# Attention start-up and the unit of the roots: one copy and the weight splits change places, and the odd query projection, sums and key spread of the first pair come later

## What is computed

```
q = (rms_norm(q_a, q_a_norm_g) @ w_uq).reshape(b, l, 16, 96)
kv = (rms_norm(kv_a, kv_a_norm_g) @ w_ukv).reshape(b, l, 16, 64 + 64)
k_nope, v = split(kv); k = concat([k_nope, broadcast(k_rope_raw)])
q = rms_norm(q, q_norm_g); k = rms_norm(k, k_norm_g)        # per head and token
q, k = rope on the last 32 features of each
s = q @ k.T * 96 ** -0.5, causal; p = softmax(s); out = p @ v
g_ssd, g_mla = split(sigmoid(gates + gate_b))               # gates = h @ w_in
x = x + (g_ssd * (y_ssd @ w_ssd_proj) + g_mla * (out @ w_mla_proj)) @ w_o
```

## Time and profile before

| | us |
|---|---|
| median of 3 runs | 1775.56 |
| the profiled execution's own time | 1777.97 |
| its span, first to last instruction | 1776.2 |
| PE busy | 1687.0 (95%) |
| DVE busy | 1069.2 (60%) |
| ACT busy | 814.2 (46%) |
| POOL busy | 628.5 (35%) |

### The profile page before, as it was taken

One profiled execution on the slowest core, in us unless ns is written; L12 is line 12 of the kernel. 1 busy time (PEld: TensorE's weight loads), 2 busy tenths in 40 slices (PEclk: granted clock), 3 DMA queues, 4 the chain that ended last, 5 costly groups with the idle time before them and its releaser, 6 DMA issues.

```text
span 1776.2 us, 22696 instructions
## 1 busy us (share of the span) xinstructions
PE 1687.0 (95%) x7979; PEld 1321.7 (74%) x7979; DVE 1069.2 (60%) x1659; ACT 814.2 (46%) x1344; POOL 628.5 (35%) x275
## 2 busy tenths in 40 slices
PE   7999899999999799999997999999999999999999
PEld 5688677767787688776675876677678788888887
DVE  6599377676526677777778026676656656666300
ACT  5432366656334355566564225554643344444310
POOL 4244211232444144344353332221224344444442
PEclk9999899999998899999999999999999899999999
DMA  6233221221432233211112221111123223233331
GB/s 203 62 95 95 77 66 48 60 72 49 153 103 87 90 96 107 66 53 36 48 46 85 76 79 48 47 52 45 60 85 108 82 93 96 94 94 96 105 95 59
DMA packets 40119, 142.72 MB, mean 80 GB/s; under 512 B 4696, under 2 KB 5176, under 8 KB 39648
## 3 DMA queue, kind: packets, MB, share of 16 engines
q1 hardware_dynamic: 37600, 131.96, 24.3%
q10 hardware_dynamic: 2432, 9.59, 1.5%
HBM read 137.31 MB, written 4.21 MB: 80 GB/s over the span
## 4 chain that ended last, share of the span: by engine, by line
PE 77%; DVE 13%; ACT 5%; issue 4%; POOL 0%; ACTq 0%; DVEq 0%; POOLq 0%
PE bank L700 16%; PE bank L702 15%; PE bank L701 15%; PE bank L1290 4%; PE bank L1289 4%; PE bank L1288 4%; PE bank L1184 1%; PE bank L751 1%; PE bank L753 1%; PE bank L752 1%; PE bank L1096 1%; PE bank L841 1%; PE bank L1205 1%; PE bank L859 1%; PE bank L1193 1%
## 5 line engine op out<-in xcount | busy, mean ns | idle before, releaser
L591 POOL TENSOR_TENSOR w_lo<-w_raw,w_hi 128x1024 fp32r<-128x1024 f32 x243 | 590.9, 2435 | 1108.8 <-ACT w_hi L1310 963.3
L700 PE MATMUL bank<-u_hi,w_hi 128*128 128x512 f32 x776 | 328.9, 424 | 14.0 <-DVE taps L2285 9.0
L1310 ACT ACTIVATE w_hi<-w_raw 128x1024 fp32r<-128x1024 f32 x199 | 208.3, 1055 | 226.9 <-PE bank L702 184.6
L702 PE MATMUL bank<-u_hi,w_lo 128*128 128x512 f32 x776 | 307.5, 396 | 0.0
L701 PE MATMUL bank<-u_lo,w_hi 128*128 128x512 f32 x776 | 307.2, 396 | 0.0
L700 PEld LDWEIGHTS bank<-u_hi,w_hi 128*128 128x128 f32 x776 | 148.4, 191 | 77.4 <-issue 30.5
L702 PEld LDWEIGHTS bank<-u_hi,w_lo 128*128 128x128 f32 x776 | 148.1, 191 | 32.7
L701 PEld LDWEIGHTS bank<-u_lo,w_hi 128*128 128x128 f32 x776 | 148.7, 192 | 29.9 <-issue 3.4
L1288 PE MATMUL bank<-u_hi,w_hi 128*128 128x512 f32 x320 | 124.5, 389 | 0.0
L1289 PE MATMUL bank<-u_lo,w_hi 128*128 128x512 f32 x320 | 124.5, 389 | 0.0
L1290 PE MATMUL bank<-u_hi,w_lo 128*128 128x512 f32 x320 | 124.5, 389 | 0.0
(11 more groups left out here) (463 smaller groups left out, 3548.6 us busy)
## 6 DMA issues: line engine op xcount, KB each, us to landing
w_raw<-weights SPq DMA_DIRECT2D x243, 512.0 KB, 3.6
xt<-x_t SPq DMA_DIRECT2D x8, 256.0 KB, 6.2
hank<-bias_dram ACTq DMA_DIRECT2D x8, 256.0 KB, 3.1
xt<-x_t ACTq DMA_DIRECT2D x1, 2048.0 KB, 9.3
h_dram<-h_res ACTq DMA_DIRECT2D x1, 2048.0 KB, 7.0
h_res<-h_dram ACTq DMA_DIRECT2D x1, 2048.0 KB, 7.7
out<-h_res SPq DMA_DIRECT2D x8, 256.0 KB
p_val<-p_t ACTq DMA_DIRECT2D x1, 512.0 KB, 11.4
```

Source lines behind the costliest of these rows:

```text
L591: pool.tensor_tensor(w_lo[:, j, :], w_raw[:, j, :], w_hi[:, j, :].bitcast(F32), ALU.subtract).then_inc(w_lo_ready, 1)
L700: pe.matmul(o, hi, xh, start=(i == 0), stop=False)
L702: mm = pe.matmul(o, lo, xh, start=False, stop=(i == n - 1))
L1310: act.activation(w_hi[:, c % RING, :], w_raw[:, c % RING, :], ACT.Copy).then_inc(w_hi_ready, 1)
```

## The change

PE's program for pair 0: the odd query projection stands behind 7 instead of 4 steps of the last output tile; its sums, the key sums and the odd sums follow after 9 and 12 steps instead of 4 and 10; the first value tile now stands ahead of the key spread, and the first gate tile has two steps instead of one before the second value tile. ACT computes one exponential of a constant behind the roots of pair 0, which brings the table in there. In the loop ACT leaves out the copy of unit i = 3 wherever a further pair follows, and DVE makes that copy ahead of the reciprocal of the roots. The split of unit i = 2 moves to unit i = 4, in every pair.

```diff
@@ PE, pair 0 @@
-            column_tile(last_out, of_y, part=(0, 4))
+            column_tile(last_out, of_y, part=(0, 7))
             project_query(1)
+            column_tile(last_out, of_y, part=(7, 9))
             query_sums(0)
-            column_tile(last_out, of_y, part=(4, 10))
+            column_tile(last_out, of_y, part=(9, 12))
             key_sums(0)
             query_sums(1)
-            column_tile(last_out, of_y, part=(10, 16))
+            column_tile(last_out, of_y, part=(12, 16))
+            row_tiles(st["v"][0:4], of_kn)
             key_spread(0)
-            row_tiles(st["v"][0:4], of_kn)
-            column_tile(gate0, of_u2, part=(0, 1))
+            column_tile(gate0, of_u2, part=(0, 2))
             row_tiles(st["v"][4:8], of_kn)
-            column_tile(gate0, of_u2, part=(1, 3))
+            column_tile(gate0, of_u2, part=(2, 3))
@@ ACT @@
             head_norms(0)
+            act.activation(norm_col[:, 2, 1:2], vec("eps"), ACT.Exp)
             scan_out(7)
...
-                head_turned(n)
-                if i == 2:
+                if i != 3 or not more:
+                    head_turned(n)
+                if i == 4:
                     after(st["head_q"][2 * p + 3] if more else st["mix_gate"][2 * p])
@@ DVE @@
                     if i == 3:
+                        dve.wait_ge(x_turn, n + 1)
+                        if n >= 4:
+                            dve.wait_ge(x_sum, n // 2 - 1)
+                        dve.tensor_copy(turned_x[:, n % 4, 0:(ti + 1) * P],
+                                        bank[6][:, 0:(ti + 1) * P]).then_inc(x_turned_out, 1)
                         head_scales(p + 1)
```

## The result

The changed kernel takes 1782.48 us (median of 20 runs, 1775.85 to 1787.6), the kernel before 1775.16 us (20 runs, 1772.8 to 1777.74): a ratio of 1.0038, 95% interval 1.003 to 1.0046. It is slower by 7.3 us where 1.4 us faster was forecast, and lies outside the range. The profiled execution took 1784.96 us, its span is 1782.8 us (before 1776.2), its mean granted clock 0.976.

What follows compares the result with a forecast made beforehand. PE, with 77% of the chain of waits, was taken as the bound. Start-up -3.6, clock +1.4, loop 0, last pair +0.85 sum to -1.35 us: 1774.2 from 1775.56, range 1770.5 to 1779.0.

Steps and rivals of the forecast that it cites:

- Odd query projection: Start-up, PE: three more output steps cover the 1.88 us q_s wait; start at 1039.8, 3.4 us of clock loss spared.
- Key spread and v_tok: Start-up: spread at 1053.0, second value tile at 1058.6, 2.5 us earlier, PE waiting about 3.1 us for v_tok.
- Fall of the clock behind that wait: Second value tile: clock down for 3.4 us after the v_tok wait, costing 1.4 us.
- clock stays up: Rival, start-up: no fall of the clock behind the 3.1 us v_tok wait; 1772.8 us, chance 0.15.
- Exponential ahead: Start-up, ACT: early table load removes PE's 0.92 us probs_x wait and more; gain 1.1 us, between 0.9 and 1.6.
- Loop, k_s for turned_x: Attention loop, PE: the 3.0 us of turned_x waits turn into k_s waits, so the gain is counted as 0.
- With DVE 0.04 us ahead it slips in between the two halves ... I take 0 for it: Loop, unit 5: DVE's probs_x rescaling starts 0.04 us before POOL's second half and is not held; cost 0.
- port lock lost: Rival, loop: POOL's second half starts just ahead of DVE's rescaling; 4.6 us lost, 1778.8 us, chance 0.28.
- The last pair: Last pair: moving the split to unit 4 makes ACT about 1.0 us later; PE loses 0.85 us, lower end 0.

Runs made afterwards that it cites:

- loop_only: The changed kernel with PE's old order ahead of the loop and without the early exponential; 1782.22 us, ratio 1.0035 to the kernel before.
- copy_only: The kernel before with one edit, DVE instead of ACT copying the transposes of unit 3; 1774.26 us, ratio 1.0001.
- last_pair_back: The changed kernel with the last pair's split in unit 2 again; 1779.15 us, ratio 1.003 to the kernel before.
- startup_only: The kernel before with only the start-up's edits, PE's new order for pair 0 and the early exponential; 1772.13 us, ratio 0.9983.
- split_later: The changed kernel with one 128x1 ACT copy ahead of the splits of unit 4; 1775.91 us, ratio 1.0001 to the kernel before.
- combined_2: The changed kernel with pair 0's key spread before the first value tile, small ACT copies ahead of unit 4's splits, last pair's split in unit 2; 1767.85 us.
- spread_first: The changed kernel with the key spread of pair 0 ahead of the first value tile; 1778.5 us, ratio 1.002 to the kernel before.
- split_unit3: The changed kernel with the splits behind the roots in unit 3, last pair as changed; 1775.26 us, ratio 0.9998 to the kernel before.

## Why the prediction was wrong

By its own steps:

- Odd query projection: right. It started at 1039.74 without a wait (predicted 1039.8), clock 1.00 from 1040 to 1050 (0.66 before).
- Key spread and v_tok: right in kind and size. (The 0.235 us a matmul was read from 1061.07 to 1063.65, which is the second value tile and not the first; the first runs at the same pace.) Spread at 1052.93 (predicted 1053.0), second value tile at 1058.49 (1058.6), wait 2.89 (3.1). It was priced as part of the start, not seen as a loss that a place ahead of the first value tile would avoid: that place gave 4.0 us.
- Fall of the clock behind that wait: right, 3.4 us. Both falls follow the waits in all traces: the one 8 us after the key projection is in the three traces with the 1.88 us wait (before, loop_only, copy_only) and in no other; the one 25 us after it is in the six with the 2.89 us wait and not in the four with 0.22. The rival "clock stays up" fell.
- Exponential ahead: 1.0 us in the start of the loop (predicted 1.1).
- Loop, k_s for turned_x: right in kind. The price of 0 should have been -0.26 us for a pair without a fall of the clock, about 1 us in sum.
- **The step that failed** is "With DVE 0.04 us ahead it slips in between the two halves ... I take 0 for it". The tally put the two starts where they were measured, POOL's second half 5.73 us behind the spread and the rescaling 5.71, but partly by luck: its terms add up to 1.62 + 0.4 + 0.3 + 1.14 = 3.46, not 3.4, which would have put POOL at 5.81 and the lead at 0.09. What failed is the price: a lead of 0.02 us did not win. DVE was held for the whole of POOL's half in six pairs, and in pair 6, where POOL starts 0.28 us sooner, too. That cost 4.9 us (loop_only against before, with what the copy gives already taken off), where the rival "port lock lost" had 4.6. The mechanism of that rival is what happened; its condition, a POOL start ahead of DVE's, held in pair 6 alone.
- The last pair: 0.77 (predicted 0.85). In last_pair_back, with the split back in unit 2, it is gone.

With 4.9 us in place of 0 the forecast would have been 1779.1. Most of the rest is the clock: the prediction counted 2.0 us less for it (3.4 saved, 1.4 spent). Over all runs the changed kernel's mean clock is 0.9779 and that of before 0.979, which is 79.0 us at the lower level against 74.4, so 2.3 us more time. That term was off by 4.3 us. Both together make 1783.4, 0.9 above the 1782.5 measured, which is as close as these estimates go. The top of the range, 1779.0, is the lost lock alone (1778.8): it left no room for a clock that came out worse as well. startup_only has 67.3 us at the lower level, and its whole gain is there: at full clock it equals before. Why the trace of the changed kernel has one more fall in its loop and one at 1320 us that startup_only has not, is not settled. Its loop has PE standing still 4.7 us more, but loop_only has these waits too, with 74.1 us of low clock.

The Trainium skill, "SBUF — State Buffer", section "Who interferes with whom", says that whoever issues first gets the shared ports for its whole instruction. In split_later and combined_2 the measurement agrees: in all 13 pairs with DVE 0.10 to 0.12 us ahead it is POOL's half that is longer, by 0.25 us. Where the lead is smaller, a reading of the rule by the starts in the profile fails: in the first six pairs of the changed kernel, loop_only, spread_first and last_pair_back, 24 in all, DVE began 0.01 to 0.03 us ahead and was the one held each time, for 2.2 us. The measurement decides: between an engine that ends one instruction and has the next one queued, and another that arrives in that moment, starts in the profile do not tell who wins below a lead somewhere between 0.03 and 0.10 us. Which instant in an instruction takes or frees the lock isn't shown by these runs. In both cases DVE's start lies inside POOL's first half, by 0.07 us in the changed kernel and by 0.16 in pair 5 of split_later, where the rescaling is none the longer for it.

## What to carry to other kernels

Where two engines exclude each other, a tally that puts one of them ahead by less than 0.1 us is no ground for a price of 0, and the price of losing belongs in the forecast; if the order is written by hand, move the off-path instruction well clear (here the splits of unit 2, with POOL 3.7 us ahead), rather than trust a lead. When a step is moved later to spare a wait, follow what hangs on it: the key spread behind twelve matmuls spared no wait that a trace shows and cost a 2.89 us wait and a fall of the clock. Read a kernel's mean granted clock over all its runs beside its time: here time x clock told work from clock to about 1 us where medians of five runs were off by 2. It is an estimate all the same: in split_unit3 the product itself scatters by 1.6 us (standard deviation), where the others have 0.3 to 1.0.

## What the runs showed of the hardware that was not expected

- A DVE rescaling that starts 0.01 to 0.03 us ahead of POOL's next queued instruction was held for all of it (2.69 us instead of 0.49), in each of the 24 pairs of four traces that had this lead. A lead of 0.10 us was enough in each of 13.
- When DVE wins, POOL's half is lengthened by 0.25 us (2.63 against 2.38), half the 0.49 us that DVE takes.
- A product of two tiles in SBUF (y_ssd from gm and y_ssd, 128x512) is held by POOL as the rescalings are: 2.31 us at 1149.61 in combined_2, where such a product takes 0.68 at 1160.88 in the changed kernel with POOL idle. The Trainium skill, "SBUF — State Buffer", section "Who interferes with whom", says that two inputs in SBUF are enough to contend with a GpSimd instruction that reads there; these rows agree.
- One added ACT copy of 128x1 in each of seven pairs made the program 6.6 us faster (split_later against the changed kernel), as it moved POOL by 0.1 us.
